# Opening of a transformer block: w_mod in row tiles of scale and shift together, pieces between the rows of x, and another order of sums, turns and splits

## The reference

```python
mod = silu(c) @ w_mod + b_mod                 # w_mod is 2048 x 12288
sh1, sc1, g1, sh2, sc2, g2 = split(mod, 6)
h = rms_norm(x, pre_mix_norm) * (1.0 + sc1) + sh1
proj = h @ w_in                               # 2048 x 9728
q_a, k_a, v_a, f_b, q_b, i_b, g_b, gate_a, gate_b = split(proj)
```

## Time and profile before

| | |
|---|---|
| median of 3 runs | 2694.45 us (2693.99 to 2694.71) |
| the profiled execution | 2694.89 us, its span 2693.2 us |
| PE busy | 2627.2 us, 98% of the span |
| DVE busy | 2076.5 us, 77% |
| ACT busy | 1158.4 us, 43% |
| mean DMA rate | 180 GB/s |

### The profile page before, as it was taken

One profiled execution on the slowest core, in us unless ns is written; L12 is line 12 of the kernel. 1 busy time (PEld: TensorE's weight loads), 2 busy tenths in 40 slices (PEclk: granted clock), 3 DMA queues, 4 the chain that ended last, 5 costly groups with the idle time before them and its releaser, 6 DMA issues.

```text
span 2693.2 us, 40797 instructions
## 1 busy us (share of the span) xinstructions
PE 2627.2 (98%) x14114; PEld 2208.3 (82%) x14114; DVE 2076.5 (77%) x3029; ACT 1158.4 (43%) x1553; POOL 210.7 (8%) x334
## 2 busy tenths in 40 slices
PE   5999999999999999999989999999999999999998
PEld 4788888888788888888878888888888888888886
DVE  7956666666766666626657999999999999988988
ACT  4344444444622222223244444444444444454454
POOL 0030000000000000002300111111111111111000
PEclk8999999999999999999999999999999999999999
DMA  9932322332277777736852665565656565988894
GB/s 361 339 112 86 86 80 84 87 87 83 67 226 216 215 219 218 218 98 227 273 157 86 168 158 143 148 152 138 162 129 163 136 156 200 329 299 304 312 319 171
DMA packets 477847, 485.64 MB, mean 180 GB/s; under 512 B 24603, under 2 KB 381234, under 8 KB 475040
## 3 DMA queue, kind: packets, MB, share of 16 engines
q1 hardware_dynamic: 442160, 384.87, 47.3%
q0 software_dynamic: 25664, 94.93, 11.8%
q10 hardware_dynamic: 9904, 4.26, 0.6%
HBM read 428.28 MB, written 34.75 MB: 172 GB/s over the span
## 4 chain that ended last, share of the span: by engine, by line
PE 90%; DVE 5%; DMA 1%; issue 1%; ACT 1%; SPq 1%; DVEq 0%; POOL 0%; ACTq 0%
PE acc_bank L849 15%; PE acc_bank L851 14%; PE acc_bank L850 14%; PE acc_bank L1280 8%; PE acc_bank L1284 4%; PE bank_tb L1280 3%; PE bank_pb L1280 3%; PE bank_ta L1280 3%; PE two_banks L1280 3%; PE two_banks L849 2%; PE two_banks L850 2%; PE two_banks L851 2%; PE bank_ta L1284 1%; PE bank_tb L1284 1%; PE two_banks L1284 1%
## 5 line engine op out<-in xcount | busy, mean ns | idle before, releaser
L840 DVE TENSOR_TENSOR w_lo<-raw,w_hi 128x1024 fp32r<-128x1024 f32 x215 | 263.0, 1223 | 370.8 <-ACT w_hi L834 370.8
L834 ACT CAST w_hi<-raw 128x1024 fp32r<-128x1024 f32 x215 | 225.4, 1049 | 540.4 <-PE acc_bank L851 379.6
L849 PE MATMUL acc_bank<-h_hi,w_hi 128*128 128x512 f32 x1124 | 447.5, 398 | 7.5 <-DVE h_lo L2007 7.5
L851 PE MATMUL acc_bank<-h_hi,w_lo 128*128 128x512 f32 x1124 | 439.5, 391 | 0.0
L850 PE MATMUL acc_bank<-h_lo,w_hi 128*128 128x512 f32 x1124 | 439.1, 391 | 0.0
L849 PEld LDWEIGHTS acc_bank<-h_hi,w_hi 128*128 128x128 f32 x1124 | 211.7, 188 | 51.4 <-issue 7.6
L851 PEld LDWEIGHTS acc_bank<-h_hi,w_lo 128*128 128x128 f32 x1124 | 211.6, 188 | 45.1
L850 PEld LDWEIGHTS acc_bank<-h_lo,w_hi 128*128 128x128 f32 x1124 | 211.9, 188 | 41.6
L1280 PE MATMUL acc_bank<-h_pair,s_hi 128*128 128x512 f32 x640 | 160.3, 393 | 0.0
L1993 DVE SCALAR_TENSOR_TENSOR acc<-raw,csil,acc 128x512 f32<-128x512 f32 x180 | 135.0, 750 | 11.8 <-DMA raw<-in_w_mod_dram 7.6
L1280 PEld LDWEIGHTS acc_bank<-h_pair,s_hi 128*128 128x128 f32 x640 | 115.2, 189 | 20.4
(11 more groups left out here) (730 smaller groups left out, 6352.9 us busy)
## 6 DMA issues: line engine op xcount, KB each, us to landing
raw<-in_w_in_dram SPq DMA_DIRECT2D x148, 512.0 KB, 4.0
raw<-in_w_mod_dram SPq DMA_DIRECT2D x96, 512.0 KB, 4.5
raw<-in_w_ffn_up_dram SPq DMA_DIRECT2D x92, 512.0 KB, 5.0
raw<-in_w_ffn_down_dram SPq DMA_DIRECT2D x86, 512.0 KB, 6.1
raw_odd<-in_w_ffn_up_dram SPq DMA_DIRECT2D x80, 512.0 KB, 5.1
raw_more<-in_w_ffn_down_dram SPq DMA_DIRECT2D x63, 512.0 KB, 5.9
mods_low<-in_w_mod_dram SPq DMA_DIRECT2D x32, 512.0 KB, 10.2
raw<-in_w_out_dram SPq DMA_DIRECT2D x32, 512.0 KB, 4.4
```

The lines of the kernel that those rows point to most:

```text
L834: act.copy(w_pair(g, gp)[0][:], raw[n % RAW][:]).then_inc(hi_ready, 1)
L840: dve.tensor_tensor(w_l[:], raw[n % RAW][:], w_h[:].bitcast(F32), ALU.subtract).then_inc(lo_ready, 1)
L849: pe.matmul(o, stat[0], mov[0], start=start, stop=False)
L851: return pe.matmul(o, stat[1], mov[0], start=False, stop=stop)
```

## The change

- A w_mod piece is now one row tile of scale and shift together, 128 x 2 x 512, and DVE's product is one instruction of 1024 (`mod_product`), alternating between two sums of 1024. Sixteen pieces make a chunk of both vectors. There are as many pieces and bytes as before, and half as many products; `MODS_HEAD` is now 32, half their number, so that the later code counts on from them.
- SP issues x rows 0 and 1, a w_mod piece, row 2, a piece, row 3. The first loads of w_in move behind pieces 12 and 15 of chunk 0.
- The diagonals come after the fifth product. The copies of the vector columns move from DVE to ACT, the start of the bounds' computation to the end of DVE's loop.
- The turns 11 to 15 come after the sums of chunk 0, with ACT's copies between its modulate steps.
- The column steps come after product 2, 3 and 3 of the next chunk, one for both vectors.
- The second iq piece comes ahead of the fourth kv piece and the first half of q. PE waits for `h_ready` tile by tile instead of piece by piece. Sums of chunks 2 and 3 stand between halves of pieces F0 and IQ2.
- The low part of pieces 0 to 11 is made within DVE's loop; before it was that of 0 to 13.
- The turns of v move behind the second half of f and into other banks; the second half of q goes to `SC1`.

```diff
-                ("kv", 2), ("q", 0), ("kv", 3), ("iq", 1), ("f", 0),
-                ("kv", 4), ("g", 0), ("kv", 5), ("iq", 2),
-                ("kv", 6), ("kv", 7), ("iq", 3), ("q", 1), ("f", 1), ("g", 1)]
-LOAD_AFTER = {1: 0, 3: 1, 10: 2, 20: 3, 23: 4, 26: 5, 30: 6, 38: 7, 42: 8, 45: 9, 48: 10, 52: 11, 55: 12, 58: 13, 61: 14}
-SPLIT_AFTER = {13: 0, 15: 1, 18: 2, 24: 3, 27: 4, 30: 5, 34: 6, 43: 7, 46: 8, 49: 9, 52: 10, 56: 11, 59: 12, 62: 13}
-SUM_BEFORE = {2: 2, 3: 3, 4: 4, 6: 5, 9: 6, 11: 7}
+START_PIECES = [("kv", 0), ("kv", 1), ("iq", 0), ("kv", 2), ("iq", 1), ("kv", 3), ("q", 0), ("f", 0), ("kv", 4), ("g", 0),
+                ("kv", 5), ("iq", 2), ("kv", 6), ("kv", 7), ("iq", 3), ("q", 1), ("f", 1), ("g", 1)]
+KV0, KV1, IQ0, KV2, IQ1, KV3, Q0, F0, KV4, G0, KV5, IQ2, KV6, KV7, IQ3, Q1, F1, G1 = range(START)
+LOAD_AFTER = {(0, 12): KV0, (0, 15): KV1, (1, 7): IQ0, (1, 12): KV2, (1, 15): IQ1, (2, 3): KV3, (2, 6): Q0, (2, 9): F0,
+              (2, 12): KV4, (3, 0): G0, (3, 3): KV5, (3, 7): IQ2, (3, 11): KV6, (3, 13): KV7, (3, 15): IQ3}
+SPLIT_AFTER = {(1, 1): KV0, (1, 5): KV1, (1, 11): IQ0, (2, 1): KV2, (2, 5): IQ1, (2, 8): KV3, (2, 10): Q0,
+               (2, 13): F0, (3, 1): KV4, (3, 8): G0, (3, 10): KV5, (3, 12): IQ2}
+COLUMNS_AFTER = 2, 3, 3
...
+            def load_mod(ch, i):
+
+                j = ch * KT + i
                 if j >= MODS_IN:
-                    sp.wait_ge(mod_ops, 2 * (j - MODS_IN) + 2)
-                sp.dma_start(MODS_SLOTS[j % MODS_IN], w_mod_t[:, 2 * i:2 * i + 2, col:col + 512]).then_inc(mod_landed[j % MODS_IN], 16)
-                if j in LOAD_AFTER:
-                    load_start(LOAD_AFTER[j])
+                    sp.wait_ge(mod_ops, j - MODS_IN + 1)
+                both_vectors = w_mod_t[:, i, :].rearrange("p (s n) -> p s n", n=D)[:, 0:2, ch * 512:ch * 512 + 512]
+                sp.dma_start(MODS_SLOTS[j % MODS_IN], both_vectors).then_inc(mod_landed[j % MODS_IN], 16)
+                if (ch, i) in LOAD_AFTER:
+                    load_start(LOAD_AFTER[ch, i])
+
+            load_x(0)
+            load_x(1)
+            load_mod(0, 0)
+            load_x(2)
+            load_mod(0, 1)
+            load_x(3)
+            for i in range(2, KT):
+                load_mod(0, i)
+            for ch in range(1, CHUNKS):
+                for i in range(KT):
+                    load_mod(ch, i)
...
+            pe.wait_ge(xn_ready, TT)
+            turn_x(0, 11)
+            chunk_sums(0, 0)
+            chunk_sums(0, 1)
+            turn_x(11, KT)
+            kv_piece(KV0)
+            kv_piece(KV1)
+            iq_piece(IQ0, 0, 4)
+            chunk_sums(1, 0)
+            chunk_sums(1, 1)
+            kv_piece(KV2)
+            iq_piece(IQ1, 0, 4)
+            kv_piece(KV3)
+            half_piece(Q0, 0, 8)
+            chunk_sums(2, 0)
+            half_piece(F0, 0, 4)
+            chunk_sums(2, 1)
+            half_piece(F0, 4, 8)
+            kv_piece(KV4)
+            half_piece(G0, 0, 8)
+            kv_piece(KV5)
+            chunk_sums(3, 0)
+            iq_piece(IQ2, 0, 2)
+            chunk_sums(3, 1)
+            iq_piece(IQ2, 2, 4)
+            kv_piece(KV6)
+            kv_piece(KV7)
+            iq_piece(IQ3, 0, 4)
+            half_piece(Q1, 0, 8)
+            half_piece(F1, 0, 8)
+            pe.wait_ge(kv_out, 4)
+            for i in range(TT):
+                for b in range(2):
+                    t = pe.transpose(v_turn(i)[:, b * P:(b + 1) * P], kvT[:, 2 + b, i * P:(i + 1) * P], ident[:])
+            t.then_inc(v_turned, 1)
+            half_piece(G1, 0, 8)
...
+            act.wait_ge(vec_turned, 2)
+            for j, rows in ((1, 72 + FB), (2, 2 * FB), (3, FB)):
+                t = act.copy(vec[:, j, 0:rows], SC1[:, j * P:j * P + rows])
+            t.then_inc(vec_ready, 1)
+            take_x(0, 11)
+            split_start(KV0, KV1)
+            act.wait_ge(cols_ready, 1)
+            act.wait_ge(xT_ready, 4)
+            modulate(0)
+            take_x(11, 13)
+            modulate(1)
+            take_x(13, 15)
+            modulate(2)
+            take_x(15, KT)
+            modulate(3)
             act.wait_ge(xT_ready, KT)
-            split_start(2)
-            modulate_chunk(0)
-            split_start(3, 4, 5, 6)
-            modulate_chunk(1)
-            split_start(7)
-            take_partial(0, 4)
-            split_start(8, 9)
+            split_start(IQ0, KV2)
+            act.wait_ge(cols_ready, 2)
+            modulate(4)
+            modulate(5)
+            split_start(IQ1)
+            modulate(6)
+            modulate(7)
+            split_start(KV3, Q0, F0, KV4)
+            take_partial(0, Q0)
             modulate_chunk(2)
-            split_start(10)
-            take_partial(1, 7)
-            split_start(11, 12)
-            take_partial(2, 9)
-            split_start(13)
+            split_start(G0)
+            take_partial(1, F0)
+            split_start(KV5, IQ2)
+            take_partial(2, G0)
             modulate_chunk(3)
-            split_start(14, 15, 16)
-            act.wait_ge(multiplied, 14)
+            split_start(KV6, KV7, IQ3, Q1)
+            act.wait_ge(multiplied, KV7 + 1)
             for b in range(4):
                 act.copy(kvT[:, b, :], KV_BANKS[b][:]).then_inc(kv_out, 1)
-            split_start(17)
-            act.wait_ge(multiplied, 15)
+            split_start(F1)
+            act.wait_ge(multiplied, IQ3 + 1)
             act.copy(iraw[:], TA[:]).then_inc(E["i_ready"], 1)
             act.copy(qh[:], TB[:]).then_inc(E["q_ready"], 1)
+            split_start(G1)
...
+            def mod_product(ch, n):
+
+                j = ch * KT + n
+                w = MODS_SLOTS[j % MODS_IN].rearrange("p v n -> p (v n)")
+                dst = mod_sums(ch)[n % 2]
+                dve.wait_ge(mod_landed[j % MODS_IN], 16 * (j // MODS_IN + 1))
+                if n < 2:
+                    if ch >= 2:
+                        dve.wait_ge(mod_summed, ch - 1)
+                        dve.wait_ge(x_turned, KT)
+                    return TS(dst, w, csil[:, n:n + 1], None, ALU.mult).then_inc(mod_ops, 1)
+                dve.wait_ge(mod_ops, j - 1)
+                return STT(dst, w, csil[:, n:n + 1], dst, ALU.mult, ALU.add).then_inc(mod_ops, 1)
...
+            def chunk_sums(ch, v):
+
+                if ch >= 2:
+                    pe.wait_ge(mod_taken, ch - 1)
+                pe.wait_ge(mod_ops, KT * (ch + 1))
+                for n in range(4):
+                    lo = (4 * v + n) * P
+                    for h, src in enumerate(mod_sums(ch)):
+                        t = pe.matmul(chunk_cols(ch, v)[:, n:n + 1], src[:, lo:lo + P], ones[:, 0:1], start=h == 0, stop=h == 1)
+                if v == 1:
+                    t.then_inc(mod_summed, 1)
...
+                dve.wait_ge(mod_summed, ch + 1)
+                lo = 4 * ch
+                for v, first in enumerate((MOD_SH1, MOD_SC1)):
+                    t = TTe(modc[:, first + lo:first + lo + 4], chunk_cols(ch, v), bmod_c[:, first + lo:first + lo + 4], ALU.add)
+                t.then_inc(mod_taken, 1)
+                dve.wait_ge(mod_taken, ch + 1)
+                STT(a1[:, 0, lo:lo + 4], modc[:, MOD_SC1 + lo:MOD_SC1 + lo + 4], 1.0, pre_mix_c[:, lo:lo + 4], ALU.add, ALU.mult
+                    ).then_inc(cols_ready, 1)
...
+            for ch in range(CHUNKS):
+                for n in range(KT):
+                    mod_product(ch, n)
+                    if ch == 0 and n == 4:
+                        diagonals()
+                    if ch and n == COLUMNS_AFTER[ch - 1]:
                         columns(ch - 1)
-                    if 3 <= i <= 6:
-                        h_low(4 * (ch - 1) + i - 3)
-                if j in SPLIT_AFTER:
-                    split_lo(dve, SPLIT_AFTER[j], SPLIT_AFTER[j])
-            columns(3)
-            for kb in range(12, 16):
+                    low = n - COLUMNS_AFTER[ch - 1] - 1
+                    if ch and 0 <= low < 4:
+                        h_low(4 * ch - 4 + low)
+                    if (ch, n) in SPLIT_AFTER:
+                        split_lo(dve, SPLIT_AFTER[ch, n], SPLIT_AFTER[ch, n])
+            columns(CHUNKS - 1)
+            for kb in range(KT - 4, KT):
                 h_low(kb)
+            bounds_start()
```

More of the change, by code:

```diff
@@ L885, in mod_sum, with gain_sum @@
+            def gain_sum(half, it):
+                pe.wait_ge(mod_ops, 2 * MODS_HEAD + 16 * (half - 1) + it * 32)
+                pe.wait_ge(mod_taken, SUMS_HEAD - 2 + half + it * 2)
                 for j in range(4):
-                    for src in sums:
-                        t = pe.matmul(cols[:, j:j + 1], src[:, j * P:(j + 1) * P], ones[:, 0:1],
-                                      start=src is sums[0], stop=src is sums[-1])
+                    t = pe.matmul(SC0[:, j:j + 1], acc[:, j * P:(j + 1) * P], ones[:, 0:1], start=True, stop=True)
@@ L903, in kv_piece, with turn_x @@
[L903 to L904 removed]
+            def turn_x(lo, hi):
```

(7 more changed lines are left out.)

185 lines of the change are left out of this document (65 added, 120 removed).

## The result

The changed kernel takes 2702.87 us (median of 8 runs, 2700.67 to 2705.31); the one before took 2694.47 in the same comparison. The ratio is 1.0031, with an interval of 1.0022 to 1.0040: slower by 8.4 us, where 5.6 was forecast on 2694.45 (2700.0, range 2695 to 2704.5). The profiled execution took 2704.53 us for a span of 2702.9.

A forecast was written before the change was run, and what follows sets the result against it. PE, full for nearly the whole span, was taken as the bound. KV6 later by 2.0, its cold restart 2.0 and k 1.0 made 5.0; 0.6 for small delays gave 5.6: 2694.45 becomes 2700.0, range 2695 to 2704.5.

The forecast's parts named there:

- Up to KV2: Opening through chunk 1: KV2 starts at 77.7 against 82.98, 5.3 us ahead, still cold after 4 us of wait.
- the product step: DVE's w_mod products: two of 745 ns become one of 1024 elements, taken as 1.28 us, with 1.22 and 1.49 kept.
- The wait at G0: Chunk 2: DVE stands in the column step, G0's low part comes at 118.1, PE waits 2.3 us.
- the 2.3 us gap at G0 cold too, +2.0: Bound at G0, left out of the sum: PE also restarts cold after that wait, +2.0 us.
- The gap: Chunk 3, ahead of KV6: an 8.3 us chain after the sums with 2.7 of PE work, so 5.6 us idle.
- The cold restart of 2.0: PE restarts at half clock after the gap ahead of KV6, costing 2.0 us.
- The fetch of k: End of the opening: k is fetched only after ACT's exponent, so PE's first scores wait 1.0 us.
- the 0.6 set aside for small delays: Whole opening: the same walk through the kernel before fell 0.6 us short of its trace, so 0.6 was added.
- my case: Main forecast: slower by 5.6 us, own range +3 to +8.5, 2697.5 to 2703; chance 0.60.
- rival (c): w_mod transfers get worse, a queue place costs 1.45, KV2 comes 2.9 us later: +8.5, 2703; chance 0.15.
- (a): KV2's lead holds, DVE not late for G0, KV2 warm, KV6's gap stays: +1, 2695.5, no change; chance 0.20.
- (b): Faster by above 5.4 us, needing w_mod queue places of 1.29 or less all the way: about 2688; chance 0.05.

The follow-up runs named there:

- e11: e7 with the v transposes put back ahead of Q1, as before the change; the first scores move by 0.16 us.
- e7: e1 plus chunk 2's sums in Q0's middle and behind it; 2689.4 us, 13.5 under the changed kernel, 4.8 under the one before.
- e3: Changed kernel with both groups of chunk 2's sums together ahead of F0; median 5.0 us lower, 2.8 gained from IQ1 on.
- e6: e1 with chunk 2's column step two products later on DVE; first scores 1.0 us earlier than e1, 1.8 from IQ1 on.
- e1: Changed kernel with KV6 and KV7 split ahead of the last modulate and column steps; median 9.1 us lower, first scores 8.35 earlier.
- e2: Changed kernel with both groups of chunk 3's sums together ahead of IQ2; median 5.0 us lower, 4.8 gained from IQ1 on.
- e9: Kernel before the change, with only the splits of KV6 and KV7 moved behind the last modulation; median 4.7 us slower, first scores 4.4 later.
- e10: e7 with chunk 1's sums ahead of IQ0's last quarter and its column step one product sooner; first scores 0.4 us later than e7.
- e13: e7 with each w_mod tile multiplied in two DVE steps of 512; 4.6 us later at the first scores, 8.1 slower in the median.
- e5: e1 and e3 edits together on the changed kernel; median 12.5 us lower, first scores 8.8 earlier, 10.0 gained from IQ1 on.

## Why the prediction was right, and where its steps were off

**Up to KV2.** Turning at 25.40 (25.5 said; the ten experiments with this interleave have 24.47 to 24.93, so the hit is part luck), the fourth row of x squared at 19.01 (19.1), the product step 1275 to 1285 ns (1280 said), KV2 at 78.36 (77.7) and cold. The table in the Trainium skill's "VectorE: DVE Perf Modes", section "The TRN2 errata", gives 1.13 us for that step, and the section itself says that its row comes out too low; the traces agree with that. KV0 was 1.3 late (54.26 for 53.0): I gave the sums "perhaps more at a fallen clock" and added nothing; they ran at half clock, and the turns behind them too. This didn't reach KV2, which hangs on DVE, as e11 beside e7 shows. KV2's 0.7 is that of the product in front of its `h_low`, which started at 76.33, behind a wait of 0.44 for its piece, and not at 75.6.

**Chunk 2.** The wait at G0, 1.91 at 118.88, stood in the prediction as 2.3 at 118.1, with its cause, and e3 and e6 take it away by the two ends of that cause. What failed is the term behind it: I kept G0 warm and put "the 2.3 us gap at G0 cold too, +2.0" among the bounds. It was cold, eight matmuls 0.43 apart, +1.6. This is the term that was mis-sized: put at nothing in the sum, though it stood among the bounds.

**Chunk 3.** The gap: 5.6 said, 5.45 measured, behind a chain of 8.3 (8.3). It is confirmed from three sides: e1 takes it away (7.5 from IQ1 on, with its cold restart), e2 shortens it by moving its start, e9 makes it in the kernel before. Because the last sums ended at 137.9 and not 135.1 (the cold stretch at G0 1.6, 0.7 from KV2, 0.5 from small delays), KV6 started 4.9 late instead of 2.0. The cold restart of 2.0 was as said.

**The fetch of k.** I had it behind ACT's exponent, a wait of 1.0. It was issued at 176.70 and 177.27, ahead of the table load at 177.73, and the scores waited for nothing. This term was wrong in kind.

**The sum.** The way the loss is made was as forecast, and its size was off by terms of either sign. KV6's start 4.9 late and 2.0 for the cold restart make 6.9 of the 7.0 at the first scores, where 5.6 was said. From the one to the other: less 1.0 for k, less the 0.6 set aside for small delays, and 2.9 more at KV6 (the 1.6, 0.7 and 0.5 above, with rounding). That 5.6 and 7.0 lie as close as they do is part luck: 1.6 of the sum wasn't there and 2.9 was missing. The profiled execution ended 9.7 late and the median 8.4. The 2.7 of the profiled execution behind the first scores I don't put down to the change: in the other twelve kernels the span's distance to before, less the distance at the first scores, is between -3.6 and +2.5, and part of it comes from stretches of lower clock, which lie differently from profile to profile (granted 0.84 from 1385 to 1430 us and 0.91 from 2280 to 2300 here, 0.92 and 1.00 in the kernel before). Whether the 1.4 of the median are more than spread is open.

The 8.4 of the median lies at the upper end of the +3 to +8.5 that I gave my case, and it is also what rival (c) forecast (+8.5, 2703). So the time alone doesn't tell the two apart; the traces do. One bound doesn't come out of its own premise: with KV2's product 42 places behind 17.68, as in (c), a queue place at 1.36 or 1.42 is worth -0.8 or +1.7, not -0.6 or +0.9.

**The rivals.** (a), no change, lost because DVE was late for G0, and because KV2 was cold. (b), faster, fell with it; a floor of its kind was real, though: e10 ran into chunk 2's last product. (c), a worse feed, fell: 373 GB/s up to 83 us, as before. e13 breaks the wide step up, which the Trainium skill says may help where Vector isn't saturated and holds up others ("Perfetto Trace Analysis", section "Optimizing Scalar/DVE Operations", not the section that the prediction names). It lost 4.6 us at the first scores, so the runs speak against doing it here.

That e1 alone brings the changed kernel back to the one before, and e7 below it, shows that the gain at KV2 was real and was lost in the order of the queues behind it, not in the tiles.

## What to carry to other kernels

After a change that moves one engine's work earlier, look in each other queue for an instruction that now waits longer and list what is queued behind it that doesn't need that wait; here two conversions stood behind a wait of 8.5 us on engines with nothing to do, and moving them was worth 7.5 us in the trace and 9.1 in the median. Price a gap on PE with the slow restart behind it, and a group of very narrow matmuls as a possible slow stretch too. When a gain at one wait is gone at the end, look at the next place fed by the same engine, as with chunk 2's sums in e10. And when two kernels' single profiles are compared, count from the last point up to which their programs agree: e5 looked 0.5 better than e1 at the first scores and was 2.5 better from IQ1 on.
